# A chunked gated recurrence among four engines: six places for its levels, the norm's root on ScalarE, its loads issued by SyncE

## The reference, cut to what matters

```
qf, kf = silu(q), 1 - f;    b = cumsum(log f) within a chunk
att[t,s] = sum_d qf[t,d] kf[s,d] exp(b[t,d] - b[s,d])     (s <= t)
o     = att @ v + (qf * exp(b)) @ state
state = exp(b_last) * state + (kf * exp(b_last - b))^T @ v
o_b   = rms_norm(o, g) * silu(gate)
mix   = concat(o_a, o_b) @ even_w_out;      x = x + mix
```

## Time and profile before

| | |
|---|---|
| median of 3 runs | 2735.71 us (2735.41 to 2735.88) |
| the profiled execution | 2738.51 us, span 2736.8 us |
| mean granted TensorE clock | 0.949 |
| busy: PE, DVE, POOL, ACT | 91%, 58%, 49%, 38% of the span |
| from the attention's last output to level 0's first Exp | 677.6 to 703.8 us |
| the recurrence with its sums, to the first product of its own projection | 703.8 to 896.0 us |

### The profile page before, as it was taken

The page is one execution under the profiler, slowest core; times in us unless marked ns, Lnnn a source line. Parts: engine busy times, 40 slices in busy tenths (PEclk is TensorE's granted clock), DMA queues, the critical chain, the costliest instruction groups (busy, mean ns, idle before and its releaser), DMA issues.

```text
span 2736.8 us, 31345 instructions
## 1 busy us (share of the span) xinstructions
PE 2499.5 (91%) x11111; PEld 1985.3 (73%) x11133; DVE 1589.1 (58%) x2354; ACT 1051.3 (38%) x1741; POOL 1353.6 (49%) x770
## 2 busy tenths in 40 slices
PE   6898897788577899999999989988998999999999
PEld 4677676444576678888888877766776888888887
DVE  6478668883677544455544654656534455544472
ACT  4255687555343422232322144525443232322220
POOL 4101234886555065566655913227524566655591
PEclk8999898799789999999999999988989999999999
DMA  4211123000300111122111212112002222111211
GB/s 147 50 28 28 31 66 93 12 10 3 123 9 8 31 55 38 61 62 61 47 38 38 74 73 73 45 33 81 9 16 62 62 61 61 46 39 38 61 54 69
DMA packets 164002, 136.57 MB, mean 50 GB/s; under 512 B 22969, under 2 KB 137730, under 8 KB 163906
## 3 DMA queue, kind: packets, MB, share of 16 engines
q1 hardware_dynamic: 143058, 116.19, 14.1%
q10 hardware_dynamic: 20848, 19.14, 2.4%
HBM read 116.17 MB, written 13.63 MB: 47 GB/s over the span
## 4 chain that ended last, share of the span: by engine, by line
PE 72%; DVE 9%; issue 8%; ACT 4%; POOL 3%; ACTq 1%; DMA 0%; another core or an unknown queue 0%; DVEq 0%; POOLq 0%
PE ps L2130 21%; PE ps L2132 21%; PE ps L2131 21%; ACT signs L1200 1%; POOL diag L824 1%; PE ps L2325 1%; PE ps L2242 1%; DVE ub L2023 1%; PE ps L2485 1%; POOL cl L874 1%; PE ps L2313 1%; PE ps L2333 1%; DVE ps L1709 1%; POOL w_lo L709 1%; DVE shared L2020 1%
## 5 line engine op out<-in xcount | busy, mean ns | idle before, releaser
L2130 PE MATMUL ps<-h_hi,w_hi 128*128 128x512 f32 x1680 | 671.6, 400 | 13.6 <-POOL w_lo L727 9.7
L2131 PE MATMUL ps<-h_lo,w_hi 128*128 128x512 f32 x1680 | 660.0, 393 | 0.0
L2132 PE MATMUL ps<-h_hi,w_lo 128*128 128x512 f32 x1680 | 659.5, 393 | 0.0
L2130 PEld LDWEIGHTS ps<-h_hi,w_hi 128*128 128x128 f32 x1680 | 319.9, 190 | 83.1 <-issue 14.4
L2131 PEld LDWEIGHTS ps<-h_lo,w_hi 128*128 128x128 f32 x1680 | 320.0, 190 | 68.2 <-issue 3.9
L709 POOL TENSOR_TENSOR w_lo<-w_raw,w_hi 128x1024 fp32r<-128x1024 f32 x73 | 182.6, 2501 | 377.3 <-ACT w_hi L1210 374.8
L2132 PEld LDWEIGHTS ps<-h_hi,w_lo 128*128 128x128 f32 x1680 | 319.1, 190 | 67.9
L2020 DVE TENSOR_TENSOR x_res<-ps,x_res 128x1024 f32<-128x1024 f32 x224 | 268.8, 1221 | 115.5 <-PE ps L2132 115.5
L2001 DVE TENSOR_TENSOR u_all<-ps,u_all 128x512 f32<-128x512 f32 x112 | 77.4, 691 | 415.9 <-ACT u_all L1107 415.9
L727 POOL TENSOR_TENSOR w_lo<-w_raw,w_hi 128x1024 fp32r<-128x1024 f32 x112 | 266.8, 2401 | 104.0 <-ACT w_hi L1096 104.0
L2130 PE MATMUL ps<-w_hi,uo_hi 128*128 128x512 f32 x784 | 307.5, 392 | 2.4 <-DVE shared L2020 2.4
(11 more groups left out here) (345 smaller groups left out, 4548.7 us busy)
## 6 DMA issues: line engine op xcount, KB each, us to landing
w_raw<-in_mlp_w_up SPq DMA_DIRECT2D x64, 512.0 KB, 4.0
w_raw<-in_mlp_w_down SPq DMA_DIRECT2D x64, 512.0 KB, 3.8
w_raw<-in_even_w_in SPq DMA_DIRECT2D x23, 512.0 KB, 3.8
w_raw<-in_odd_w_in SPq DMA_DIRECT2D x10, 512.0 KB, 3.7
x_res<-in_x SPq DMA_DIRECT2D x8, 512.0 KB, 8.1
x_res<-in_x ACTq DMA_DIRECT2D x8, 512.0 KB, 8.6
scr_x<-x_res SPq DMA_DIRECT2D x8, 512.0 KB, 2.6
x_res<-scr_x SPq DMA_DIRECT2D x8, 512.0 KB, 4.4
```

The lines of the kernel that those rows point to most:

```text
L2130: t_.matmul(out_, ah, bh, start=first, stop=False)
L2131: t_.matmul(out_, ah, bl, start=False, stop=False)
L2132: return t_.matmul(out_, al, bh, start=False, stop=last)
```

## The change

- Six places for levels: `cl` keeps four, `cl2` in the last 4 KB of x's region holds two. READ_LAG goes from 3 to 5; there are still four banks.
- Nearly every constant moves (diff). In slots from a chunk's end: out and state product 1 -> 4, state update 5 -> 9, turn 6 -> 8, gate 9 -> 12, high 10 -> 13, low 11 -> 14.
- The norm of chunk d is done by ACT alone, at n = 7(d+1) + 6, in one piece: four squares with their sums, Ln, Exp (scale -0.5), and four scalings. It waits for the chunk's *state* product. DVE's sum, reciprocal and scaling go.
- The sums' first parts stand at l = 0 and 3 (before 0 and 2), DVE's additions still three slots behind; the turn of `ek` goes to bank 7.
- The 24 transfers are issued by SP, once the last attention output is computed; the last tile of x waits for the last level. The last attention block's division, high and low parts move into slots 6, 9 and 11, and nobody waits for them before slot 0.

```diff
-        RING = 4
+        RING = 6
-        L_KL_ARG, L_KL_EXP, L_KL_PROD, L_KL_TURN, L_KL_COPY = 0, 2, 3, 4, 6
-        L_QE_EXP, L_QE_PROD, L_LAST, L_SPLIT = 4, 5, 6, 6
-        R_OUT, R_SQUARE, R_STATE, R_ROOT, R_NORM, R_TURN, R_GATE, R_HIGH, R_LOW = 1, 4, 5, 6, 7, 6, 9, 10, 11
-        READ_LAG = 3
+        L_KL_ARG, L_KL_EXP, L_KL_PROD, L_KL_TURN, L_SPLIT = 2, 3, 4, 5, 6
+        R_KL_COPY, R_QE_EXP, R_QE_PROD, R_LAST = 0, 2, 2, 4
+        R_OUT, R_ROOT, R_STATE, R_TURN, R_GATE, R_HIGH, R_LOW = 4, 6, 9, 8, 12, 13, 14
+        READ_LAG = 5
+        LAST_NORM, LAST_HIGH, LAST_LOW = 6, 9, 11
-        OA_SLOTS = [7 * c + l for c in range(2, T) for l in (0, 2)] + [7 * T + l for l in (0, 2, 4, 5)]
-        OA_LAG = 3
+        OA_FIRST = [7 * c + l for c in range(2, T) for l in (-1, 2)] + [7 * T + l for l in (-1, 2, 5, 8)]
+        OA_PIECES = {n + 1: (i, (0, 1, 2, 3)) for i, n in enumerate(OA_FIRST)}
+        OA_ADDS = {n + 4: i for i, n in enumerate(OA_FIRST)}
...
                 d = after_chunk(n, R_ROOT)
                 if d is not None:
-                    act.wait_ge(hg["o_ss"], d + 1)
-                    s.activation(sd[:, 0:4], ss[:, 0:4], ACT.Sqrt, scale=1.0 / P, bias=epsc[:]) \
-                        .then_inc(hg["o_sd"], 1)
+                    act.wait_ge(hg["s_done"], d + 1)
+                    for h in range(4):
+                        hs = slice(h * P, (h + 1) * P)
+                        ins = s.activation(kf[:, d, hs], ps[:, 5, hs], ACT.Square, accum_out=ss[:, h:h + 1])
+                    own.link(ins)
+                    own.link(s.activation(sd[:, 0:4], ss[:, 0:4], ACT.Ln, scale=1.0 / P, bias=epsc[:]))
+                    own.link(s.activation(rstd[:, 0:4], sd[:, 0:4], ACT.Exp, scale=-0.5))
+                    for h in range(4):
+                        ins = s.activation(chunk_values(o_sum, d)[:, h, :], ps[:, 5, h * P:(h + 1) * P], ACT.Identity,
+                                           scale=rstd[:, h:h + 1])
+                    ins.then_inc(hg["o_norm"], 1)
                 d = after_chunk(n, R_HIGH)
                 if d is not None:
                     act.wait_ge(hg["o_full"], d + 1)
```

More of the change, by code:

```diff
@@ L377, in after_chunk, with level @@
             return c if rem == 0 and 0 <= c < T else None
+        def level(n):
+            return (cl if n % RING < 4 else cl2)[:, n % RING % 4, :]
         def chunk_values(t, c):
@@ L855, in attention @@
                     u = ends_at(layer, n - ROUND[layer])
-                    if u is not None and u % 2:
+                    if u is not None and u % 2 and (layer or u // 2 < T - 1):
                         q = u // 2
@@ L865, in _ @@
             attention(0, PF0, PH0, PL0, diag0)
-            for n in range(7 * T):
+            last_block = block_outputs(0, T - 1)
+            for n in range(7 * T + R_QE_PROD + 1):
                 c, l = divmod(n, 7)
[L868 to L881, removed]
+                if n == LAST_LOW:
+                    pool.wait_ge(att["o_hi"], T)
+                    g.tensor_tensor(h_lo[last_block], o_den[last_block], h_hi[last_block].bitcast(F32), ALU.subtract) \
+                        .then_inc(att["o_lo"], 1)
+                if c < T:
+                    B = 1 << l
+                    e = level(n).rearrange("p (m s j) -> p m s j", s=2, j=B)
+                    pairs = kq[:, 0:2 * (KQ + B)].rearrange("p (s r) -> p s r", s=2)[:, :, c * 512:(c + 1) * 512]
+                    mixed = pairs.rearrange("p s (m j) -> p m s j", j=2 * B)[:, :, :, 0:B]
+                    pool.wait_ge(hg["exp"], 2 * n + 2)
+                    g.tensor_tensor(e, e, mixed, ALU.mult).then_inc(hg["prod"], 1)
+                    if l == L_KL_PROD:
+                        pool.wait_ge(hg["kl_exp"], c + 1)
+                        g.tensor_tensor(ek[:], ek[:], kf[:, c, :], ALU.mult).then_inc(hg["kl"], 1)
+                d = after_chunk(n, R_QE_PROD)
+                if d is not None:
+                    pool.wait_ge(hg["qe_exp"], d + 1)
+                    g.tensor_tensor(qe[:], qe[:], qf[:, d, :], ALU.mult).then_inc(hg["qe"], 1)
+                if l == L_SPLIT and 2 <= c < T and c % 2:
@@ L1348, in _ @@
[L1348 to L1353, removed]
+                d = after_chunk(n, R_KL_COPY)
                 if d is not None:
-                    act.wait_ge(hg["o"], d + 1)
+                    act.wait_ge(hg["kl_turned"], d + 1)
@@ L1357, in _ @@
                     if d:
-                        act.wait_ge(hg["o_full"], d)
-                    s.activation(ps[:, 7, :], ps[:, 5, :], ACT.Square).then_inc(hg["o_sq"], 1)
+                        act.wait_ge(hg["s_done"], d)
+                    s.activation(klT[:], ps[:, 7, :], ACT.Copy).then_inc(hg["klT"], 1)
+                d = after_chunk(n, R_QE_EXP)
+                if d is not None:
+                    if d:
+                        act.wait_ge(hg["o"], d)
+                    s.activation(heads(qe[:]), bT[:, :, d * P:(d + 1) * P], ACT.Exp).then_inc(hg["qe_exp"], 1)
@@ L2520, in _ @@
                     pe.wait_ge(hg["o_norm"], d + 1)
+                    pe.wait_ge(hg["klT"], min(d + 2, T))
                     for h in range(4):
```

108 lines of the change are left out of this document (54 added, 54 removed).

## The result

| | before | after |
|---|---|---|
| median | 2735.75 us (2735.41 to 2735.88, 4 runs) | 2770.70 us (2769.47 to 2772.35, 4 runs) |
| profiled execution, its span | 2738.51, 2736.8 us | 2770.50, 2768.6 us |
| ratio of the times | | 1.0127, 95% interval 1.0112 to 1.0142 |
| first state product ends | 724.80 | 707.83 |
| second, seventh | 744.39, 865.24 | 735.70, 896.22 |

The change costs 35 us by the medians, 1.3% of the time; the forecast was 21.7 slower, 2757.4. In the profiled executions the stretch up to the own projection ends 33.0 us later, and the span is 31.8 us longer.

What follows compares the result with a forecast made beforehand. No engine is full; the loop of waits through the ordered lists bounds the kernel. Seam -20.6, first cycle +5.7, five cycles +39.0 and tail -2.4 sum to +21.7 us, from the median 2735.71 to 2757.4; range 2730 to 2770.

Steps and rivals of the forecast that it cites:

- seam, first state product: From the attention's end to the first state product: it ends at 704.2, not 724.8, so -20.6 us.
- first cycle: State products 0 to 1, without a low part: 25.3 us with handovers against 19.6, so +5.7.
- five cycles: Second to seventh state product: 32.0 us a cycle against 24.2, so 7.8 x 5 = +39.0.
- tail: Behind state product 6, up to the recurrence's own projection: 28.4 us against 30.8, so -2.4.
- steps 1 to 8: The chain of waits in a cycle from chunk 1 on, from one state product's end to the next: 31.05 us.
- 1.0 for the clock: Added per cycle for PE's lower clock behind pauses, in the first level and part of the first sum: 1.0 us.
- Step 1: ACT's norm: four squares with sums, a load, Ln, a load, Exp, four scalings; 5.8 us, 0.4 per square with read.
- Step 5: PE's level 0 of the next chunk (0.9), then first sum's first product to its addition (3.1): 4.0 us.
- The places pay: Rival, faster: DVE, not ACT, sets the cycle, about 24.5 us; six places let ACT and POOL run ahead; 2718; chance 0.13.
- One table set: Rival, no change: with Ln and Exp in one set no norm loads, 17.9 us less, 2739.5; chance 0.03.
- Cold PE: Rival, slower: a cycle of 34.5 us or more, 2770 and up; chance 0.06.
- A balance: Rival: single terms of steps 4 and 7 overlap, a cycle of 27 to 28.5 us, 2732 to 2740; chance 0.06.

Runs made afterwards that it cites:

- high_first: The changed kernel with ACT's high part of chunk c-2 put ahead of the norm of chunk c-1 in the same slot: 2736.68 us, 1.0003 to before.
- no_loads: The changed kernel with Exp in place of Ln in the norm, so no table is loaded there (output not the reference's): 2748.02 us, 1.0052 to before.
- sums_early: The changed kernel with each cycle's first sum two slots earlier on PE and its additions moved: 2743.04 us, 1.0026 to before.
- filler_both: The changed kernel with 24 unread PE products before level 6 and 14 more between the diagonal and level 0: 2760.59 us, 1.0077 to before.
- filler: The changed kernel with 24 unread PE products before each level 6 from chunk 2 on: 2769.48 us, 1.0129 to before.

## Why the prediction was right and wrong

The direction, the wait that the change adds, and most of the visible signs were right; the sum was 10 us short by the spans and 13 by the medians. One sign was not: the longest wait of DVE in all is that of the additions (67.3 us), and the low part's comes second (50.4). Against the measured marks:

| term | forecast | measured |
|---|---|---|
| seam, first state product | -20.6 | -17.0 |
| first cycle | +5.7 | +8.3 |
| five cycles | +39.0 | +39.7 |
| tail | -2.4 | +2.0 |
| sum | +21.7 | +33.0 |

**The seam** was too good by 3.6. The first Exp came at 680.26, not 678.8, and POOL's product started 1.6 us late against the forecast. Of this, 0.4 is POOL's last part of the attention, which took 1.67 us instead of 1.27, with DVE's differences beside it; 1.0 is that this part started later, at 676.32 and not 675.30; in the traces of the other versions it starts anywhere from 670.86 to 677.79. That 1.0 is no step of the forecast. POOL then had a pause of 1.38 that I had given to nobody (DVE's division in slot 6, which I had summed for DVE alone) and its own low part of 1.72, which the term left out. Its products were 1.1 us cheaper in sum. (The prediction's second count, of DVE's work, adds up to 698.9 and not to 701; nothing rests on it.)

**The five cycles** agree to 0.7 us, but not term by term. In the cycle from 800.97, steps 1 to 8 measure 5.3, 0.7, 1.35, 5.8, 6.7, 1.9, 4.0 and 7.55, sum 33.3; forecast were 5.8, 0.6, 1.35, 6.1, 4.0, 2.0, 3.95 and 7.25, and 1.0 for the clock. Step 1 was too long: a square with its read takes 0.25 us a head, not 0.4, as the next head's square overlaps the read. Step 5 was too short by 2.7, all of it PE at the lower clock: eight products 2.07 and not 0.9 to 1.13, and the first nine of the sum's twelve some 0.43 apart and not 0.23. In the last of the five cycles level 0 ran at the upper level (1.16 us) and the addition waited 4.1 us; that cycle lasts 30.2, with level 6 still at the lower. So 1.0 was too low for the clock even as a mean, the other steps were too long in sum, and the agreement to 0.7 us is in part luck. That the low part's wait costs is shown by high_first (4.8 us a cycle), the norm's loads by no_loads, the delay of the first sum by sums_early, the clock by filler_both.

**The first cycle and the tail** are where the clock was left out. The term "25.3" had no clock in it, and is what filler measured with the upper level there (24.75); after's 27.87 holds level 0 in 2.04 us and an addition 4.75 us behind the sum's first product. In the tail level 6 held PE for 1.7 us instead of 0.9 (+0.8), the addition behind it came 4.6 us after its sum's first product instead of 3.1 (+1.5), and the last sum took 5.3 instead of 2.6 (+2.7); with 0.5 less for each of two norms that is 4.0 of the 4.4 us missed:

```profile
903.63 2.08 PE L2505 MATMUL ps<-cl 128*128 128x128 f32 x8 [6.08 <-DVE acc L1999]
...
923.76 0.80 PE L2151 MATMUL ps<-w_hi,h_hi 128*128 128x512 f32 x1 [0.96 <-DVE x_res L1940]
...
929.04 0.39 PE L2151 MATMUL ps<-w_hi,h_hi 128*128 128x512 f32 x1
```

The step that failed is the size of the clock's term: priced once a cycle from the earlier trace rows, at 1.0 us, and at nothing in the two ends, where such pauses stand too and where it measured some 2.4 and 5.0 us. The seam's sum failed by less: POOL's pause and its low part, 3.1 us, were given no term. The earlier trace rows showed eight products at 1.58; behind longer pauses all of a level runs at the lower level, and most of the sum behind it. The bound of 34.5 a cycle held that; the bounds of seam and tail held nothing, and so the range ended at 2770, 0.7 short. Either of the two would have filled so small a gap.

**The rivals.** The places pay: no, at 2770.7, and neither of its conditions came true (the norm takes 5.3 us, and the low part waits). But a cycle like its 24.5 can be had by another order: with the low part out of the norm's shadow and the sums earlier it is 23.3, and there the places are worth 11 us. One table set: no, two loads stand in each norm. (There are eight norms, not seven: its price would have been 20.5 us, not 17.9.) The drain of 1.38 us a switch that the Trainium skill gives (ScalarE: Activation LUTs, What ACT_TABLE_LOAD costs) isn't seen here either: Ln follows the end of its load by 0.02 us, and the next load comes 0.01 us behind Ln. Cold PE: its number was right, by another way; the cycles stayed at 32, the clock came in at both ends. A balance: no, the cycles are over 30 us.

The profiled executions differ by 32.0 us and the medians by 35.0, as the profiled one of before was 2.8 above its median; these 3 us aren't resolved.

## What to carry to other kernels

Where an engine's long piece (here a norm of 5.3 us) is put into an ordered list, ask what short result stands behind it and who reads that first: moving one 0.6 us copy ahead of the norm gave back 34 us. More places for data in flight paid in the cycles (1.3 us each) only once the waits in the ordered lists were gone; judge them again when such a wait is removed. Split a change into its parts: the seam alone gained 20 us, and the change as a whole hid it. A mark in a trace also holds what came before it: count from the last event that the change can't have moved. If a forecast makes PE pause where it did not, price the lower clock at every pause, in the first cycle and the tail too, with bounds that hold all the work behind it: here up to eight or nine products of a sum besides the level.

## What the runs showed of the hardware

The same 3.59 us pause, after the same instructions, left PE's granted clock at the upper level (2.4 GHz: eight products 1.13 us) in one kernel and at the lower (1.2 GHz: 2.04) in another. Pauses of 2.1 us were followed by products at either level (1.16 us at 789.95 in after, 2.07 at 785.93 in filler_both). Which it is can't be told from the pause before it alone; in the first cycle the two kernels (filler and after) differ by 3.1 us. The sum of twelve products took 2.8 us at the upper level (910.69 to 913.54 in after) and 5.3 at the lower (923.76 to 929.04).

A DVE operation on two SBUF operands (128x512) took 0.69 us alone and 1.1 to 1.9 beside POOL's products: the low part had a mean of 0.69 in after, where POOL stood still in the norm's shadow, and 1.50 in before and 1.33 in high_first, where it didn't. So of what high_first won by taking the wait away, 0.64 us a low part went back.
